# Seven Strassen products in five iterations of two more up projections of a two-block transformer kernel

## What is computed

```
def conv_ffn(xn, w_up, conv_w, w_down):           # layers 0 and 1
    up = xn @ w_up                                # 1024 x 5632
    a, g = jnp.split(up, 2, axis=-1)
    a = causal_dwconv(a, conv_w)                  # 3 taps along the positions
    return (jax.nn.silu(a) * g) @ w_down
...
    gu = h2 @ w_ffn_in[l]                         # layer 2, 1024 x 5632
    ff_gate, ff_up = gu[..., :D_FF_2], gu[..., D_FF_2:]
    x = x + (jax.nn.silu(ff_gate) * ff_up) @ w_ffn_out[l]
```

## Time and profile before

| what | value |
|---|---|
| median of 3 runs | 2090.46 us |
| the profiled execution | 2090.37 us |
| its span, first to last instruction | 2088.6 us |
| TensorE busy | 2074.1 us, 99% |
| GpSimd busy | 1512.6 us, 72% |
| VectorE busy | 1026.3 us, 49% |
| ScalarE busy | 546.0 us, 26% |
| mean granted TensorE clock | 0.998 |
| share of TensorE in the chain that ended last | 95% |

### The profile page before, as it was taken

How to read it: one execution, slowest core, us unless ns; L and a number is a source line. 1 busy time by engine, 2 the same in 40 slices (tenths; PEclk the granted TensorE clock), 3 DMA queues, 4 the chain that set the end, 5 groups by cost and what they waited for, 6 DMA issues and landing times.

```text
span 2088.6 us, 28877 instructions
## 1 busy us (share of the span) xinstructions
PE 2074.1 (99%) x10328; PEld 1741.3 (83%) x10328; DVE 1026.3 (49%) x1527; ACT 546.0 (26%) x1085; POOL 1512.6 (72%) x1551
## 2 busy tenths in 40 slices
PE   9999999999999999999999999999999999999999
PEld 8888888888788888888888888989888888897887
DVE  6566655522456675755541176546643256663100
ACT  2002111100366773211110053222452124441000
POOL 7888888868865447888877775556546796887675
PEclk9999999999999999999999999999999999999999
DMA  5333333323332223333323332223222233333333
GB/s 158 100 91 104 93 98 98 93 86 97 101 109 82 83 80 87 100 91 100 99 78 103 94 96 71 71 62 101 81 61 81 81 111 94 89 102 90 86 91 96
DMA packets 368176, 192.63 MB, mean 92 GB/s; under 512 B 8672, under 2 KB 364608, under 8 KB 368080
## 3 DMA queue, kind: packets, MB, share of 16 engines
q1 hardware_dynamic: 365280, 186.52, 30.9%
q10 hardware_dynamic: 2800, 4.83, 0.7%
HBM read 189.19 MB, written 2.13 MB: 92 GB/s over the span
## 4 chain that ended last, share of the span: by engine, by line
PE 95%; DVE 2%; ACT 1%; POOL 1%; issue 0%; DMA 0%; SPq 0%; DVEq 0%; ACTq 0%; POOLq 0%
PE PS L641 20%; PE PS L642 20%; PE PS L643 20%; PE PS L1012 3%; PE PS L1014 3%; PE PS L1013 3%; PE PS L1028 2%; PE PS L1029 2%; PE PS L1030 2%; PE PS L854 1%; PE PS L856 1%; PE PS L855 1%; PE PS L748 1%; PE PS L747 1%; PE PS L749 1%; PE PS L733 1%
## 5 line engine op out<-in xcount | busy, mean ns | idle before, releaser
L624 POOL TENSOR_TENSOR RING<-RAW,RING 128x512 fp32r<-128x512 f32 (+1 forms) x656 | 909.1, 1386 | 54.7
L621 POOL TENSOR_SCALAR RING<-RAW 128x512 fp32r<-128x512 f32 (+1 forms) x656 | 482.0, 735 | 361.1 <-PE PS L1014 90.1
L641 PE MATMUL PS<-XH,RING 128*128 128x512 f32 x1104 | 430.9, 390 | 5.1 <-POOL RING L624 5.1
L642 PE MATMUL PS<-XL,RING 128*128 128x512 f32 x1104 | 430.2, 390 | 0.0
L643 PE MATMUL PS<-XH,RING 128*128 128x512 f32 x1104 | 430.0, 389 | 0.0
L641 PEld LDWEIGHTS PS<-XH,RING 128*128 128x128 f32 x1104 | 207.6, 188 | 49.9 <-issue 6.6
L643 PEld LDWEIGHTS PS<-XH,RING 128*128 128x128 f32 x1104 | 207.6, 188 | 43.3
L642 PEld LDWEIGHTS PS<-XL,RING 128*128 128x128 f32 x1104 | 207.6, 188 | 43.0 <-issue 0.2
L641 PE MATMUL PS<-HH,RING 128*128 128x512 f32 x528 | 205.6, 389 | 0.0
L643 PE MATMUL PS<-HH,RING 128*128 128x512 f32 x528 | 205.4, 389 | 0.0
L642 PE MATMUL PS<-HL,RING 128*128 128x512 f32 x528 | 205.4, 389 | 0.0
(11 more groups left out here) (386 smaller groups left out, 3941.6 us busy)
## 6 DMA issues: line engine op xcount, KB each, us to landing
RAW<-in_ffn_w_up SPq DMA_DIRECT2D x88, 512.0 KB, 3.6
RAW<-in_w_in SPq DMA_DIRECT2D x52, 512.0 KB, 3.5
RAW<-in_w_ffn_in SPq DMA_DIRECT2D x44, 512.0 KB, 3.7
RAW<-in_ffn_w_down SPq DMA_DIRECT2D x32, 512.0 KB, 3.7
RAW<-in_a_w_in SPq DMA_DIRECT2D x24, 512.0 KB, 3.6
RAW<-in_b_w_qg SPq DMA_DIRECT2D x16, 512.0 KB, 3.9
RAW<-in_w_kvf SPq DMA_DIRECT2D x16, 512.0 KB, 3.8
RAW<-in_w_ffn_out SPq DMA_DIRECT2D x16, 512.0 KB, 3.7
```

The costliest lines, as they stand in the source:

```text
L621: hi = pool.tensor_scalar(WH[s][:, k0_:k1, :], RAW[r][:, k0_:k1, :], 1.0, 1.0, ALU.mult, ALU.mult)
L624: lo = pool.tensor_tensor(WL[s][:, k0_:k1, :], RAW[r][:, k0_:k1, :], WH[s][:, k0_:k1, :].bitcast(F32), ALU.subtract)
L641: pe.matmul(o, WH[s][:, k, :], xh[:, k0 + k, :], start=first and k == 0, stop=False)
L642: pe.matmul(o, WH[s][:, k, :], xl[:, k0 + k, :], start=False, stop=False)
```

## The change

- Layers 0 and 1 get a seven-product stretch too: iterations 2 to 6 in each (`SEVEN` becomes a dictionary). Layer 2 keeps iterations 2 to 7.
- In layers 0 and 1 the combined tiles go through the convolution before silu, two times three VectorE instructions per iteration. Silu waits for the convolution.
- Entry: the half passes of plain iterations 0 and 1 and the making of the operands are interleaved in another order on VectorE and ScalarE. TensorE waits for the low part of each operand by itself, no more for all four at once. The first copy out of bank 0 (`keep_first`) moves ahead on ScalarE, before the high part of tile 3 and use 6.
- Exit: the first plain unit after a stretch takes the ring slot that comes free first (`first`), which is slot 1 in layer 2 and slot 0 in layers 0 and 1.
- Scratch tiles move, since layers 0 and 1 hold other data in W7 and W9; the count for a narrow weight load is derived instead of written out.

```diff
-SEVEN = range(2, 8)
+SEVEN = {0: range(2, 7), 1: range(2, 7), 2: range(2, 8)}
...
-            c = wphase(4, FT // 2 - SEVEN.stop, plain, start=SEVEN.stop)
-            return a, b, c
+            first = (last + 1) // 2 % 4
+            c = wphase(4, FT // 2 - SEVEN[l].stop, plain, first, start=SEVEN[l].stop)
...
                         elif t == 0:
                             if q < 4:
                                 pe.wait_ge(sem(("ffn_a", "ffn_g")[q % 2]), m - 1 + q // 2)
-                            if q == 1:
-                                pe.wait_ge(sem("xld"), scaled(4) + KT + 4)
+                            if q in (1, 2, 3, 5):
+                                pe.wait_ge(sem("seven_added"), earlier(l, 3, 8) + T_COUNT[{1: 1, 2: 2, 3: 0, 5: 3}[q]])
...
                     high(0, 0)
+                    operand_high(0)
+                    operand_high(1)
                     silu(0, 1)
                     high(0, 1)
-                    operands_high()
+                    operand_high(2)
+                    round_use(0)
+                    round_use(1)
                     silu(1, 0)
-                    round_use(0)
                     high(1, 0)
-                    round_use(1)
+                    operand_high(3)
                     round_use(2)
                     round_use(3)
                     silu(1, 1)
                     round_use(4)
                     round_use(5)
+                    keep_first(0)
                     high(1, 1)
                     round_use(6)
...
                         for q in range(2):
-                            dve.tensor_tensor(u[q], u[q], W[0][:, 0:S], ALU.mult).then_inc(sem("ffn_a"), 1)
+                            dve.tensor_tensor(a[q], a[q], W[0][:, 0:S], ALU.mult).then_inc(sem("ffn_a"), 1)
+                            if with_conv:
+                                dve.wait_ge(sem("ffn_a"), m + q + l * FT + 1)
+                                convolve(m + q, q).then_inc(sem("ffn_u"), 1)
...
-                if l == 2:
-                    body(0)
-                    operands(0)
-                    operands(1)
+                if l in SEVEN:
+                    half(0, 0)
+                    operand(0)
+                    operand(1)
                     operand_low(0)
-                    operands(2)
+                    half(0, 1)
+                    operand(2)
                     operand_low(1)
-                    operands(3)
                     operand_low(2)
+                    add_weights(0)
+                    half(1, 0)
+                    operand(3)
                     operand_low(3)
-                    body(1)
+                    half(1, 1)
                     seven()
```

More of the change, by code:

```diff
@@ L427, in seven_phases, with add_ffn, is_seven, earlier @@
                         t, q = divmod(n, SEVEN_USES)
-                        of.append(b.unit(SEVEN.start + t, 1 if q < 7 else 2 + (q - 7) // 2))
+                        of.append(b.unit(b.start + t, 1 if q < 7 else 2 + (q - 7) // 2))
                 stream["owner"][slot] = max(of)
-            c = wphase(4, FT // 2 - SEVEN.stop, plain, start=SEVEN.stop)
-            return a, b, c
+            first = (last + 1) // 2 % 4
+            c = wphase(4, FT // 2 - SEVEN[l].stop, plain, first, start=SEVEN[l].stop)
+            d = []
+            for q in range(2):
+                d += [(down[l], k0, min(KT, FT - k0), col(q * P, 2 * P)) for k0 in (0, 8, 16)]
+            return a, b, c, wphase(3, KT // 2, d, first)
+        sevens = list(SEVEN)
+        narrow_count = [None]
+        def add_ffn(l):
+            if l < 2:
+                stream["loads"][3] += 1
+                narrow_count.append(stream["loads"][3])
+            if l in SEVEN:
+                ph[f"up{l}"], ph[f"seven{l}"], ph[f"rest{l}"], ph[f"down{l}"] = seven_phases(l)
+            else:
+                ph[f"up{l}"], ph[f"down{l}"] = ffn_phases(l)
+        def is_seven(p):
+            return p in [ph[f"seven{l}"] for l in sevens]
+        def earlier(l, each, more=0):
+            return sum(more + each * len(SEVEN[o]) for o in sevens[:sevens.index(l)])
         ph = {}
@@ L564, in body @@
                                 load_parameters()
-                if p is ph["seven2"]:
-                    for i in SEVEN:
+                if is_seven(p):
+                    for i in range(p.start, p.start + p.iters):
                         body(i)
@@ L589, in _, with seven_low @@
             pool.wait_ge(sem("zeroed"), 2)
[L591 to L593 removed]
+            def seven_low(l):
+                for t in range(len(SEVEN[l])):
                     for q in range(SEVEN_USES):
@@ new lines, in seven_operands, with operand_high, keep_first @@
+                    cp.then_inc(sem("taken"), 1)
+                def operand_high(c):
+                    act.wait_ge(sem("seven_added"), earlier(l, 3, 8) + TF_COUNT[c])
+                    act.copy(TH[:, c], TF[1 + c][:, :, :]).then_inc(sem("taken"), 1)
+                def keep_first(t):
+                    act.wait_ge(sem("used"), used_count(l, t, 1))
+                    if t > 0:
+                        act.wait_ge(sem("combined"), combined_count(l, t - 1, 5))
+                    act.copy(P1U2[l][:, 0], PS[:, 0, 0:HALF]).then_inc(sem("taken"), 1)
@@ L2044, in add_weights, with operand @@
                     dve.tensor_tensor(a21, a11, a21, ALU.subtract).then_inc(sem("seven_added"), 1)
-                def operands(part):
+                def operand(part):
                     if part == 0:
-                        dve.wait_ge(sem("xhd"), scaled(n) + KT + 1)
+                        dve.wait_ge(sem("taken"), operand_count(l, 1))
                     b12, n1, t2, t3, t4 = TF
-                    g = [PRM[:, R_FFN2 + k:R_FFN2 + k + 1] for k in range(KT)]
+                    row = (R_FFN, R_FFN + KT, R_FFN2)[l]
@@ new lines, in seven @@
+                        dve.tensor_tensor(a[1][:, HALF:S], U3, PS[:, 3, 0:HALF], ALU.subtract).then_inc(done, 1)
+                        dve.wait_ge(sem("used"), used_count(l, t, 6))
+                        dve.tensor_tensor(a[1][:, 0:HALF], PS[:, 4, 0:HALF], U3, ALU.add).then_inc(done, 1)
+                        if t + 1 < len(SEVEN[l]):
+                            add_weights(t + 1)
+                        dve.wait_ge(unit_done, ph[f"seven{l}"].unit(i, 1) + 1)
+                        if not with_conv:
+                            dve.wait_ge(sem("ffn_h"), l * FT + m)
@@ L2136, in ffn @@
-                    loop(dve, FT // 2, body, steps, start=SEVEN.stop)
+                    pu = ph[f"rest{l}"]
+                    loop(dve, FT // 2, body, steps, start=SEVEN[l].stop)
                 else:
```

251 lines of the change are left out of this document (132 added, 119 removed).

## The result

The changed kernel takes **2124.43 us** (median of 4 runs, 2124.01 to 2125.5) against 2090.47 us (2090.38 to 2091.24, 4 runs): ratio 1.0162, 95% interval 1.0147 to 1.0177, so 1.6% slower. The prediction was 2126.8 with a range of 2104 to 2147. The profiled execution took 2125.5 us, its span is 2123.7, and the mean granted clock of TensorE 0.992.

A forecast was written before the change was run, and what follows sets the result against it. TensorE, 99% busy, was taken as the bound. Each new layer: 11.4 + 14.9 + 1.5 - 3.9 = +23.9; two layers +47.8, layer 2 -11.4, together +36.4 on span 2088.6, plus 1.8 around it: 2126.8 us, range 2104 to 2147.

The forecast's parts named there:

- Term 1: New stretches: each seven-product iteration saves 0.78 us; ten more give -7.8 us, 3.9 per layer, if TensorE sets the pace.
- Term 2: Layer 2's entry and exit: removing their losses gives -11.4 us together, bounds -12 to -7.
- I leave 0.5 us: Layer 2's entry: loss remaining out of 4.9 us once the first copy of bank 0 comes earlier.
- ends just as TensorE asks for it: Layer 2's entry: the chain of weight sums and operands, by the same durations, finishes just in time.
- Term 3: Loop through the new stretches: a turn takes 24.7 us against TensorE's 20.98, +14.9 us per layer, bounds +5.3 and +29.
- All alone: 6.3: Turns in layers 0 and 1: scaling and convolution take 6.3 us if undisturbed, against the 8.7 assumed.
- before products 4 and 5: Turns in layers 0 and 1: where TensorE would stand, 3.7 us in each of four turns, waiting for GpSimd.
- Term 4: Entries of layers 0 and 1: VectorE's added work makes TensorE wait, +11.4 us per layer, bounds +7 and +14.
- Term 5: Lower clock after pauses, in the last iteration of each new layer's stretch: +1.5 us per layer, bounds 0 and 3.
- A: Rival: VectorE mostly undisturbed in layers 0 and 1, turn 22 us, entry 9; total 2099.4 us; chance 14%.
- C: Rival: new work hidden, turn at or under 20.98 us, entry at most 4; faster, 2079 us; chance 8%.
- B: Rival: tighter chain with blocked instructions, or slow clock in turns; turn 27.5 us or more, 2149 and up; chance 10%.

The follow-up runs named there:

- experiment 5: Changed kernel with one convolution instruction in place of three per tile in the stretches of layers 0 and 1 (work left out): 2097.0 us.
- experiment 6: Changed kernel with one VectorE instruction in place of four per operand sum in layers 0 and 1 (work left out): 2112.02 us.
- experiment 7: Changed kernel with the edits of experiment 5 and experiment 6 together: 2085.82 us, ratio 0.9976.
- experiment 1: Changed kernel without the new stretches of layers 0 and 1; layer 2's new entry and exit stay: 2081.17 us, ratio 0.9954.
- experiment 8: As experiment 1, but the first plain unit after the stretch goes into ring slot 0 again: 2088.83 us, ratio 0.9991.
- experiment 3: Changed kernel with the next iteration's copy out of bank 0 (keep_first) moved ahead of use 6 on ScalarE: 2123.97 us.
- experiment 2: Changed kernel with ScalarE making uses 3 to 5 ahead of both silus, use 6 between them, in layers 0 and 1: 2124.24 us.
- experiment 4: Changed kernel with the stretches of layers 0 and 1 starting at iteration 3, one seven-product iteration less each: 2119.76 us.
- experiment 9: As experiment 1, with ScalarE making uses 2 and 3 before the fourth operand's high part, use 4 before the second silu: 2081.63 us.

## Why the prediction was right, and where it was not

**The total.** 2126.8 forecast, 2124.43 measured, the mechanism is the forecast one: the loop through the convolution, and the entry. Experiments 5 to 7 show both, and that they add up. That the total is within 2.4 us is in part luck: over eight turns the chain was forecast 4.7 us too long, and 4.1 us that TensorE adds to it hid most of that; layer 2 came out 2.0 us worse, and 1.5 us outside the stretches were not foreseen.

**Term 1, the products.** -0.78 us an iteration holds: where nothing holds TensorE up, iterations of the new stretches take 20.98 us (experiment 5).

**Term 2, layer 2.** -11.4 forecast, -9.4 by the trace and -9.3 by experiment 1. The exit was right (-7.0 forecast, -7.7 by experiment 8). The failed step is "I leave 0.5 us" at the entry: 2.5 are left, two waits of 0.7 and 1.2 us for GpSimd and 0.6 at the restarts, at full clock. The old wait for the copy went, and GpSimd and VectorE's half pass were next, a step that the sentence "ends just as TensorE asks for it" should have priced.

**Term 3, the turns.** 24.7 us forecast; at TensorE 24.46 measured in layer 0 and 24.8 in layer 1; 14.9 forecast per layer, 13.9 and 15.2 measured. The chain itself, between SP's issues, took 24.1 in both layers, so it was 0.6 a turn too high. TensorE's four turns sum to more than the chain's four (97.9 against 96.5, and 99.1 against 96.4), which hid most of that error: in layer 0 this is so at full clock too (experiment 3, 98.3), in layer 1 1.6 of it went when the clock stayed up. Scaling and convolution 8.7 forecast, 8.3 measured, GpSimd's part 5.9 in place of 6.3. The first tile took 4.6 us (259.89 to 264.5) where 4.4 was forecast, the second 3.7 in place of 4.1. The 0.87 us that the prediction took for L2008 and L2009 alone is too long: the same instructions took 0.75 in the kernel after (L2071, L2072), so "All alone: 6.3" should have been some 5.9. The method carried this: the old chain was timed as a whole by two issues of the same queue, so only the one inserted piece had to be estimated. The **place of the wait** was wrong: TensorE stands ahead of product 4 only, released by the copy of bank 0, not "before products 4 and 5" by GpSimd. That the copy is queued on ScalarE behind uses 6 and 7 could have been read from the order. It cost nothing in the sum: experiment 3 moved it and the time stayed.

**Term 4, the entries.** +11.4 forecast, 10.6 and 11.1 measured. Timeline of VectorE at the entry of layer 0, kernel after: the reads of `a` and `g` of tile 2 and of tile 3, and the fourth operand between them:

```profile
230.41 0.69 DVE L2182 TENSOR_TENSOR W<-PS,W 128x512 f32<-128x512 f32 x1
...
233.75 0.69 DVE L2188 TENSOR_TENSOR W<-PS,W 128x512 f32<-128x512 f32 x1
...
236.59 1.67 DVE L2126 SCALAR_TENSOR_TENSOR TF<-XT,PRM,TF 128x256 f32<-128x256 f32 x4
...
240.59 0.68 DVE L2182 TENSOR_TENSOR W<-PS,W 128x512 f32<-128x512 f32 x1
...
244.46 0.68 DVE L2188 TENSOR_TENSOR W<-PS,W 128x512 f32<-128x512 f32 x1
```

They end at 231.1, 234.4, 241.3 and 245.1 where the prediction had 231.0, 234.7, 241.8 and 246.0. The long wait is 5.63 us before product 2, forecast 5.7. Its last link is another than forecast. The row of that wait names GpSimd; timeline of ScalarE and GpSimd, same kernel, the high part of the fourth operand, the high part of use 2 and its low part:

```profile
238.29 1.05 ACT L1544 CAST TH<-TF 128x1024 fp32r<-128x1024 f32 x1 [2.34 <-DVE TF L2126]
239.25 0.61 ACT L1531 CAST RING<-RAW 128x512 fp32r<-128x512 f32 x1
...
239.94 1.85 POOL L650 TENSOR_TENSOR RING<-RAW,RING 128x512 fp32r<-128x512 f32 x1 [7.95 <-ACT RING L1531]
```

Use 2 is queued on ScalarE behind the fourth operand, its low part ends at 241.79, and product 2 starts at 241.84; the read of `a` of tile 3, which the prediction names, was done 0.5 us earlier. Both paths start at VectorE's fourth operand, so the number came out. The other waits are smaller than forecast (0.5, 0.5 and 1.1 in place of 1.1, 2.6 and 2.0). The first is so because product 0 starts 0.25 us later and `g` of tile 2 is read 0.3 us earlier; for the second, product 2 itself takes 2.7 us in place of 1.44 at the lower clock (0.84 over the entry). In all the 10.6 us are 7.7 of waits, 2.0 of products 2 and 3 at the lower clock and 0.9 at the restarts.

**Term 5, the clock.** "+1.5 per layer" did not appear as a term behind the others: the slow clock lies inside the entry and the turns, whose measured lengths hold it (2.0 us in layer 0's entry; in the turns 1.6 us in layer 1 and none in layer 0, by experiment 3). Its source was read a little wrong too: the pause at the old entry is 2.9 us by the earlier trace rows, not 3.1. Beside the measured lengths the term is 3.0 us too much over both layers; the entries were 1.1 and the turns 0.7 too high, layer 2 was 2.0 too low, and the 1.5 us outside the stretches were not foreseen: 3.0 + 1.1 + 0.7 - 2.0 - 1.5 = 1.3, the difference of the spans (2125.0 and 2123.7).

**Rivals.** A and C needed a shorter chain, which only experiments 5 and 7 made, by leaving work out. B's place was half right: VectorE and GpSimd do slow each other to 23.4 us a turn, but only when the chain doesn't keep them apart (experiment 2). The Trainium skill's rule (SBUF — State Buffer, Who interferes with whom) agrees in its direction: of the convolution's three instructions the two with two SBUF inputs more than double beside GpSimd (0.75 to 1.66 us). The same section counts a multiplication by a column of factors (`tensor_scalar`) among those that can take both ports when their operands meet its conditions, and the row of L2074 above agrees with that too, with 1.40 us as the mean of eight beside GpSimd and 0.49 in the earlier trace rows.

**What stays open.** 1.0 of the 1.5 us outside the stretches, and what remains of the entries (5.4 and 5.5 us) in experiments 6 and 7. No run moves the fourth operand behind the read of `a` of tile 3 in layers 0 and 1, though product 2 doesn't need that operand and stands behind its 4.0 us on VectorE: the entry's order is an untested remedy, at the same work. That experiment 2 met VectorE's limit is shown by its idle time of 1.0 us a turn; a kernel with both the late silu and less work beside it wasn't run.

## What to carry to other kernels

Before a scheme that saves TensorE columns is put on a stretch, find the loop that goes round the other engines once per iteration, time it as a whole by two issues of the same load in a trace of its present use, and add the new pieces: it gave 24.7 here where 24.1 was measured, and each microsecond over TensorE's pace comes back every turn. Room on an engine is what it idles per iteration, not the length of the iteration, less what a neighbour's extra work costs it, and a chain that is broken by reordering may only uncover the next limit (24.1 by the chain, 23.4 by VectorE); ask for that limit before the edit. Take a change's parts apart: here the entry and the exit alone are 0.43% faster, and the rest only hides it.

## What the hardware showed that was not expected

- A VectorE multiplication by a column of factors, 128x512 in float32, took 0.49 us while GpSimd was idle and 1.40 beside a GpSimd instruction (L2070, L2074); the two-input forms went from 0.69 or 0.75 to 1.66. The first I had taken as undisturbed. Twice this price undid a gain: 6.8 us in experiment 4 and 2.1 in experiment 9.
- In layer 0 a pause of 3 to 4 us before a product makes a slow iteration and then a short one (26.8, 22.9, 26.8, then 21.4 us); the same loss spread over shorter waits, at clock 1.00, gives 24.4 each, and the same total within 0.4 us. There the lower clock after a pause cost nothing, since TensorE had to wait for the chain anyway; in layer 1, where the last turn ran at 0.93, the kernel with the short waits was 1.6 us shorter.
